# Turning the gated activations of the four plain FFNs in 32x32 blocks on VectorE, with ScalarE moving the pieces

## What is computed

```
def _swiglu(x, wg, wu, wd):
    return (jax.nn.silu(x @ wg) * (x @ wu)) @ wd
# per plain FFN: x is (256, 1024), wg and wu are (1024, 2816), wd is (2816, 1024)
h = h + FFN_RES * _rmsnorm(_swiglu(_rmsnorm(h, g[0]), ffn1_wg[i], ffn1_wu[i], ffn1_wd[i]), g[1])
```

## Time and profile before

| | us |
|---|---|
| median of 3 runs | 1398.85 (1398.45 to 1399.58) |
| the profiled execution's own time | 1399.31 |
| its span in the trace | 1397.5 |
| PE busy | 1379.0 (99%) |
| DVE busy | 874.7 (63%) |
| ACT busy | 752.1 (54%) |
| granted TensorE clock, mean | 1.00 |

### The profile page before, as it was taken

One profiled execution on the slowest core, in us unless ns is written; L12 is line 12 of the kernel. 1 busy time (PEld: TensorE's weight loads), 2 busy tenths in 40 slices (PEclk: granted clock), 3 DMA queues, 4 the chain that ended last, 5 costly groups with the idle time before them and its releaser, 6 DMA issues.

```text
span 1397.5 us, 20401 instructions
## 1 busy us (share of the span) xinstructions
PE 1379.0 (99%) x6545; PEld 1143.4 (82%) x6545; DVE 874.7 (63%) x1231; ACT 752.1 (54%) x1293; POOL 116.2 (8%) x184
## 2 busy tenths in 40 slices
PE   9999999999999999999999899999999999999999
PEld 7888878878888878888888788888788898888887
DVE  6555566777555566555577865555667876676664
ACT  7444455566444465444466764444555565565553
POOL 2322110011000000000011100000013000000000
PEclk9999999999999999999999999999999999999999
DMA  9866747315655647555655446556575523555551
GB/s 291 255 197 202 220 134 252 112 46 172 211 188 181 208 126 234 184 192 183 195 190 183 128 136 224 185 190 202 173 225 167 174 69 106 195 185 180 184 190 43
DMA packets 192313, 248.44 MB, mean 178 GB/s; under 512 B 17130, under 2 KB 130038, under 8 KB 192131
## 3 DMA queue, kind: packets, MB, share of 16 engines
q1 hardware_dynamic: 188704, 242.35, 54.3%
q0 software_dynamic: 3440, 5.36, 1.5%
q10 hardware_dynamic: 115, 0.05, 0.0%
HBM read 244.40 MB, written 1.18 MB: 176 GB/s over the span
## 4 chain that ended last, share of the span: by engine, by line
PE 94%; DVE 3%; ACT 1%; issue 1%; DMA 0%; SPq 0%; ACTq 0%; DVEq 0%
PE ps L288 25%; PE ps L290 25%; PE ps L289 25%; PE ps L325 2%; PE ps L315 2%; PE ps L318 2%; PE ps L709 1%; PE ps L952 1%; PE ps L415 1%; PE ps L417 1%; PE ps L416 1%; PE ps L340 1%; PE ps L988 1%; PE ps L1325 1%; PE ps L905 1%
## 5 line engine op out<-in xcount | busy, mean ns | idle before, releaser
L281 DVE TENSOR_TENSOR wlo<-raw,whi 128x1024 fp32r<-128x1024 f32 x450 | 546.9, 1226 | 345.4 <-ACT whi L273 345.1
L273 ACT CAST whi<-raw 128x1024 fp32r<-128x1024 f32 x450 | 469.0, 1051 | 317.8 <-PE ps L290 307.5
L288 PE MATMUL ps<-whi,xhi 128*128 128x512 f32 x1188 | 466.5, 393 | 0.3 <-DVE xlo L519 0.3
L290 PE MATMUL ps<-whi,xlo 128*128 128x512 f32 x1188 | 462.6, 389 | 0.0
L289 PE MATMUL ps<-wlo,xhi 128*128 128x512 f32 x1188 | 462.3, 389 | 0.0
L290 PEld LDWEIGHTS ps<-whi,xlo 128*128 128x128 f32 x1188 | 223.0, 188 | 46.8
L288 PEld LDWEIGHTS ps<-whi,xhi 128*128 128x128 f32 x1188 | 223.1, 188 | 45.7 <-issue 0.5
L289 PEld LDWEIGHTS ps<-wlo,xhi 128*128 128x128 f32 x1188 | 223.1, 188 | 45.4
L288 PE MATMUL ps<-whi,thi 128*128 128x512 f32 x384 | 153.9, 401 | 0.0
L290 PE MATMUL ps<-whi,tlo 128*128 128x512 f32 x384 | 150.2, 391 | 0.0
L289 PE MATMUL ps<-wlo,thi 128*128 128x512 f32 x384 | 149.7, 390 | 0.0
(11 more groups left out here) (223 smaller groups left out, 1272.2 us busy)
## 6 DMA issues: line engine op xcount, KB each, us to landing
raw<-in_ffn_wg_dram SPq DMA_DIRECT2D x176, 256.0 KB, 2.9
raw<-in_ffn_wu_dram SPq DMA_DIRECT2D x176, 256.0 KB, 3.1
raw<-in_ffn_wd_dram SPq DMA_DIRECT2D x176, 256.0 KB, 3.0
raw<-in_w_ffn_up_dram SPq DMA_DIRECT2D x88, 256.0 KB, 3.6
raw<-in_w_in_dram SPq DMA_DIRECT2D x80, 256.0 KB, 3.3
raw<-in_diff_w_in_dram SPq DMA_DIRECT2D x48, 256.0 KB, 3.2
raw<-in_na_w_in_dram SPq DMA_DIRECT2D x48, 256.0 KB, 3.2
raw<-in_w_ffn_down_dram SPq DMA_DIRECT2D x44, 256.0 KB, 3.2
```

The lines of the kernel that those rows point to most:

```text
L273: nc.scalar.copy(whi[:, s], raw[:, s]).then_inc(s_hi, 1)
L281: nc.vector.tensor_tensor(wlo[:, s], raw[:, s], whi[:, s].bitcast(F32), ALU.subtract).then_inc(s_lo, 1)
L288: nc.tensor.matmul(outs[t], ahi[:, c], whi[:, s, i], start=start, stop=False)
L290: last = nc.tensor.matmul(outs[t], alo[:, c], whi[:, s, i], start=False, stop=stop)
```

## The change

For chunks 0 to 9 of each plain FFN PE no longer turns anything; `hidden_t` keeps only its wait. Chunk 10 is as before. VectorE turns all of `hs` (128 partitions x 512) with one instruction that transposes each 32x32 block in place (`turn_blocks`, into `hB`). The blocks then stand in the right orientation but in the wrong partition quadrant, and ScalarE copies them to theirs with sixteen copies of 32 partitions x 128 elements, SBUF to SBUF (`move_blocks`, into `hT`), in two groups of eight. `hidden` then reads `hT` in SBUF, no PSUM bank. `hB` and `hT` lie in parts of `qkv` that the plain FFNs did not use.

```
+        hT = qkv[:, 1, 0:512].rearrange("p (j s) -> p j s", j=2)
+        hB = qkv[:, 1, 512:1024].rearrange("p (t c) -> p t c", t=NT)
...
             def hidden_t(c):
                 pe.wait_ge(s_hc, 2 * b + 2 * c + 2)
+                if not isinstance(c, int) or c < NCH - 1:
+                    return
...
-                nc.scalar.copy(thi[:, j], ps[:, Z + 2 + j, 0:S]).then_inc(s_hth, 1)
+                nc.scalar.copy(thi[:, j], hT[:, j]).then_inc(s_hth, 1)
+
+            def move_blocks(c, rows):
+                for i in rows:
+                    for q in range(4):
+                        ins = nc.scalar.copy(
+                            hT[32 * q:32 * q + 32].rearrange("p j (t c) -> p j t c", t=NT)[:, :, :, 32 * i:32 * i + 32],
+                            hB[32 * i:32 * i + 32].rearrange("p t (j c) -> p j t c", j=2)[:, :, :, 32 * q:32 * q + 32])
+                if rows[-1] == 3:
+                    ins.then_inc(s_ht, 1)
...
-                nc.vector.tensor_tensor(tlo[:, j], ps[:, Z + 2 + j, 0:S], thi[:, j].bitcast(F32),
+                nc.vector.tensor_tensor(tlo[:, j], hT[:, j], thi[:, j].bitcast(F32),
                                         ALU.subtract).then_inc(s_htl, 1)
+
+            def turn_blocks():
+                nc.vector.transpose(hB[:], hs[:]).then_inc(s_hb, 1)
```

More of the change, by code:

```diff
@@ L242, in build @@
         s_si2 = sem("conv_silu")
+        s_hb = sem("hidden_blocks_transposed")
         s_out = sem("out_written")
@@ L734, in ffn_act @@
             swish(n0 + 3, Y)
-            for j in range(1, UP):
-                hi(act, n0 + RING + j)
+            hi(act, n0 + RING + 1)
+            act.wait_ge(s_hb, (NCH - 1) * f + 1)
+            move_blocks(0, range(2))
+            hi(act, n0 + RING + 2)
+            move_blocks(0, range(2, 4))
             hidden(0, 0)
             hidden(0, 1)
+            hi(act, n0 + RING + 3)
             def body(it):
@@ L744, in body @@
                 hi(act, n0 + RING + 7, it)
[L745 to L748, removed]
+                if not isinstance(it, int):
+                    act.wait_ge(s_hb, (NCH - 1) * f + it + 2)
+                    act.wait_ge(s_htl, 2 * b + 2 * it + 2)
+                    move_blocks(it + 1, range(2))
+                    hi(act, n0 + RING + 8, it)
+                    move_blocks(it + 1, range(2, 4))
+                    hi(act, n0 + RING + 9, it)
+                    for j in range(2):
+                        hidden(it + 1, j)
+                    return
+                hidden(it + 1, 0)
+                hi(act, n0 + RING + 8, it)
+                hidden(it + 1, 1)
             chunks(act, n0, body)
@@ L765, in hidden @@
                     return
-                nc.vector.tensor_tensor(tlo[:, j], ps[:, Z + 2 + j, 0:S], thi[:, j].bitcast(F32),
+                nc.vector.tensor_tensor(tlo[:, j], hT[:, j], thi[:, j].bitcast(F32),
                                         ALU.subtract).then_inc(s_htl, 1)
+            def turn_blocks():
+                nc.vector.transpose(hB[:], hs[:]).then_inc(s_hb, 1)
             lo(dve, n0 + RING)
             gated(0, Y)
-            for j in range(1, UP):
-                lo(dve, n0 + RING + j)
+            lo(dve, n0 + RING + 1)
+            dve.wait_ge(s_hc, 2 * b + 2)
+            turn_blocks()
+            lo(dve, n0 + RING + 2)
             hidden(0, 0)
             hidden(0, 1)
+            lo(dve, n0 + RING + 3)
             def body(it):
@@ L778, in body @@
                 gated(it + 1)
+                if not isinstance(it, int):
+                    dve.wait_ge(s_hc, 2 * b + 2 * (it + 1) + 2)
+                    turn_blocks()
                 lo(dve, n0 + RING + 7, it)
-                for j in range(2):
-                    hidden(it + 1, j)
-                    if j == 0 or not isinstance(it, int):
+                if not isinstance(it, int):
+                    for j in range(2):
                         lo(dve, n0 + RING + 8 + j, it)
+                    for j in range(2):
+                        hidden(it + 1, j)
+                    return
+                hidden(it + 1, 0)
+                lo(dve, n0 + RING + 8, it)
+                hidden(it + 1, 1)
             chunks(dve, n0, body)
```

## The result

| | before | with the change |
|---|---|---|
| median, us | 1398.85 (7 runs) | 1403.84 (1402.85 to 1405.76, 7 runs) |
| ratio | | 1.0038, interval 1.0029 to 1.0048 |
| profiled execution: its time, span | 1399.31, 1397.5 | 1404.43, 1402.6 |
| PE busy | 1379.0 | 1366.8 |
| ACT busy | 752.1 | 941.2 |

The forecast was 1390.7 in a range of 1386.0 to 1400.5; the change costs 5.0 us where it should have saved 8.1.

What follows compares the result with a forecast made beforehand. PE, busy for 99% of the span, was taken to bound the kernel. 19.2 us of removed turns, less chunk 0's stalls (23.1 - 4T - 64p), saves 8.1: 1398.85 - 8.1 = 1390.7 us, range 1386.0 to 1400.5.

Steps and rivals of the forecast that it cites:

- a turn is worth 0.48 us, not its four durations: In each chunk's four PE transposes: removing them frees 0.48 us, 19.2 us for 40, not the 43 us of summed durations.
- In the loop everything is covered: In chunks 1 to 9: the added work takes 11.9 us against a 16.32 us period, so 36 turns save in full.
- Chunk 0 is not covered: In chunk 0 of each FFN: PE waits for `gated` 3.8, 2.8, 1.5 and 2.8 us, 10.9 us in all.
- T: On VectorE: time of one block transpose of 512 elements, taken as 0.7 us, with bounds 0.45 to 1.2.
- p: On ScalarE: distance between the starts of two moves that follow each other, taken as 0.19 us.
- its formula: In chunk 0: the PE stall is T + 16p - 0.9, 2.8 us in f1, varying by FFN with silu's lateness.
- If ACT waits elsewhere than for PE: In the profile afterwards: ScalarE waiting for anything but PE was named as one sign that the forecast is wrong; no size.
- the term 64p: In chunk 0 of the four FFNs: the cost of sixteen moves each, subtracted from the saving, with p taken as 0.19.
- the sum: Over the whole kernel: saving = 23.1 - 4T - 64p, which is 8.1 us at T = 0.7 and p = 0.19.
- small copies do not overlap: Rival on ScalarE's moves: p = 0.295, or T near 1.1, so chunk 0's stalls eat the saving; 1397.4 to 1399.5; chance 0.16.
- Slower from p = 0.36: Rival in chunk 0: moves costing 0.37 us or more make PE's waits exceed the saving, 1402.2 at p = 0.37; chance 0.11.
- my own family of likely prices: For ScalarE's moves: the forecast's case, p from 0.165 to 0.26, giving 1389 to 1395 us; chance 0.56.

Runs made afterwards that it cites:

- the first experiment: The changed kernel with the change kept for chunks 1 to 9 only, chunk 0 of each plain FFN turned by PE as before: 1381.27 us, ratio 0.9876.

## Why the prediction was wrong, point by point

- *PE bounds the kernel, and a turn is worth 0.48 us, not its four durations*: right. The loop chunks went from 16.81 to 16.32; a run without moves gave 18.7 of 19.2.
- *In the loop everything is covered*: right, shown by the first experiment (17.4 saved, 17.3 expected) and by the limit measured with further copies.
- *Chunk 0 is not covered, and PE waits there for `gated`*: right in place and mechanism. T was 0.71 for 0.7. With p = 0.309 its formula gives stalls of 5.7, 4.8, 3.5 and 4.8 us in f0 to f3; the pairs of waits, with 0.15 for each that the idle time leaves out, are 5.6, 4.6, 3.4 and 4.6.
- *"If ACT waits elsewhere than for PE"* was a poor sign of being wrong: ACT waits 29.7 us in all for the block transpose (L742's row above), and the prediction's own chain has such a wait. In the loop it costs nothing.
- **The step that failed first is the term 64p.** I took p = 0.19 from the overlap of three `hi`, which all work on the same 128 partitions; it is 0.309. A single move's duration was right, 0.297 for 0.295. In the sum this is 64 x 0.119 = 7.6 us: 23.1 - 2.8 - 19.8 leaves 0.5. The prediction asked whether a change of quadrant costs and left that out of its own value. Its rival "small copies do not overlap", at 1397.4, had the mechanism and, in "writes of one quadrant after another", half of the reason: a new source quadrant alone does it, too. At the measured p and T the sum gives 1398.4, so this rival would have missed 1403.8 as well.
- **The second is missing altogether: the clock.** The prediction named PE waits of 1.5 to 3.8 us and priced them as idle time alone, at a granted clock that it had just read as 1.00. Each fall costs 1.6 us by the silu distances and 1.7 by the windows; 4.6 us of the 5.0 lost went away when the waits were filled. With the 7.6 of the moves that is 12.2 of the 13.1 us between forecast and median. The kernel with its moves kept in their quadrants shows that at about the assumed p, too, the gain would have been gone (1398.17).
- *Slower from p = 0.36*: the change did come out slower, and the rival's 1402.2 lies near 1403.8, but that is luck: it takes p = 0.37 and no fall of the clock, where p was 0.309 and the clock made up the difference. The deciding point was wrong. With the clock's 4.6 to 6.8 us the saving is gone from about p = 0.21 to 0.25, within my own family of likely prices.
- The waits' idle time was 17.0 us where the sum with p = 0.309 and T = 0.71 gives 18.7; with the 0.15 of each of the eight it is 18.2. The slower start behind a wait, 0.33 for 0.23, was in no term; eight times that is 0.8.

## What to carry to other kernels

Work moved off the bounding engine is paid for where its new engine has no slack, and that is the prologue of a loop rather than its body: cost both apart, and change the body alone if the prologue does not fit (here 17.4 us saved against 5.0 lost). An overlap between instructions read from one kind of row holds for that kind only; for small pieces on changing partitions take the whole duration. Where TensorE is the limit, a wait of two or three microseconds is to be priced with a possible fall of the clock behind it (1.6 to 1.7 us here), or filled with matmuls that nobody reads.

## What the hardware showed that was not expected

- ScalarE's copies of 32 partitions x 128 elements start 0.20 us apart if source and destination partitions are those of the copy before, and 0.31 apart if either differs, whether or not a copy crosses quadrants. `hi` (128 partitions) next to a move does not overlap either: 346.57 to 347.65 is 1.08 for a cast of 1.05.
- TensorE fell from 2.4 to 1.2 GHz behind waits of 2.08, 2.21, 2.23, 2.9 and 4.2 us that were the only ones above 0.2 us in their chunk, and stayed at 2.4 GHz behind others of 2.21, 2.88 and 2.89. Two waits per chunk of 1.3 and 1.2 us, in f2 of the kernel with further copies, never brought it down. Between these the length of the wait does not decide alone; what does stays open here.
- VectorE's transpose of 128x512 float32 in 32x32 blocks takes 0.71 us, as much as an elementwise operation of that size.
